# ScalarE instead of VectorE writes the one-hot operand of each expert's bias product

## What is computed

```python
u = xb @ w1[e] + b1[e]
glu = jnp.minimum(u[:, ::2], SWIGLU_LIMIT)
lin = jnp.clip(u[:, 1::2], -SWIGLU_LIMIT, SWIGLU_LIMIT)
a = glu * jax.nn.sigmoid(SWIGLU_ALPHA * glu) * (lin + 1.0)
return a @ w2[e] + b2[e]
```

## Time and profile before

| | before |
|---|---|
| median of 3 runs (lowest to highest) | 3779.34 us (3778.82 to 3779.49) |
| the profiled execution's own time | 3781.95 us |
| its span | 3780.1 us |
| TensorE, VectorE, ScalarE busy over the span | 91%, 55%, 46% |
| one unit of the mixture | some 36.5 us, 34 of them |

### The profile page before, as it was taken

One profiled execution on the slowest core, in us unless ns is written; L12 is line 12 of the kernel. 1 busy time (PEld: TensorE's weight loads), 2 busy tenths in 40 slices (PEclk: granted clock), 3 DMA queues, 4 the chain that ended last, 5 costly groups with the idle time before them and its releaser, 6 DMA issues. The chain is left out here.

```text
span 3780.1 us, 55651 instructions
## 1 busy us (share of the span) xinstructions
PE 3444.3 (91%) x20889; PEld 2782.7 (74%) x20889; DVE 2088.5 (55%) x2469; ACT 1755.3 (46%) x2286; POOL 1040.9 (28%) x435
## 2 busy tenths in 40 slices
PE   7989999969999999999999687899998886779997
PEld 4877777648888888888887574688877765668876
DVE  2320111259999999999999236411240263246665
ACT  3222333137787777777777325222242342033333
POOL 2334233202322223232231220244432300024443
PEclk9999999969999999999999798799998966789999
DMA  8223433249999999999999327123231200013221
GB/s 270 80 67 95 138 114 123 78 152 366 366 381 370 370 380 365 383 366 375 376 365 374 116 82 267 45 78 100 95 95 56 96 1 5 7 46 101 100 86 43
DMA packets 245432, 696.84 MB, mean 184 GB/s; under 512 B 17846, under 2 KB 149802, under 8 KB 186652
## 3 DMA queue, kind: packets, MB, share of 16 engines
q1 hardware_dynamic: 234956, 657.73, 46.7%
q0 software_dynamic: 9936, 36.18, 3.6%
q10 hardware_dynamic: 384, 0.65, 0.0%
HBM read 668.73 MB, written 30.23 MB: 185 GB/s over the span
## 5 line engine op out<-in xcount | busy, mean ns | idle before, releaser
L311 POOL TENSOR_TENSOR split_w<-ring,split_w 128x1024 fp32r<-128x1024 f32 (+1 forms) x294 | 698.2, 2375 | 1736.7 <-ACT split_w L306 1589.5
L1811 DVE TENSOR_TENSOR moe_low<-ring,moe_high 128x2048 fp32r<-128x2048 f32 x408 | 929.1, 2284 | 23.6 <-ACT moe_high L1802 23.4
L1802 ACT ACTIVATE moe_high<-ring 128x1024 fp32r<-128x1024 f32 x810 | 827.7, 1058 | 103.7 <-PE psum L2054 101.8
L306 ACT ACTIVATE split_w<-ring 128x1024 fp32r<-128x1024 f32 (+1 forms) x294 | 304.7, 1036 | 1034.6 <-PE psum L376 649.2
L2050 PE MATMUL psum<-moe_high,moe_xe 128*128 128x512 f32 x2176 | 586.9, 391 | 0.0
L2050 PEld LDWEIGHTS psum<-moe_high,moe_xe 128*128 128x128 f32 x2176 | 410.4, 189 | 85.2
L1962 POOL DMA_INDIRECT moe_y_rows<-moe_ye,moe_target x34 | 197.4, 5806 | 696.2 <-DVE moe_ye L1866 696.2
L376 PE MATMUL psum<-pair,split_w 128*128 128x512 f32 x1584 | 364.7, 393 | 13.0 <-PEq L128 6.2
L376 PEld LDWEIGHTS psum<-pair,split_w 128*128 128x128 f32 x1584 | 300.5, 190 | 76.5 <-issue 9.1
L376 PE MATMUL psum<-b_pair,split_w 128*128 128x512 f32 x1440 | 334.7, 394 | 12.9 <-PEq L840 7.1
L2054 PE MATMUL psum<-moe_low,moe_xe 128*128 128x512 f32 x1088 | 337.3, 391 | 0.0
(11 more groups left out here) (589 smaller groups left out, 4336.9 us busy)
## 6 DMA issues: line engine op xcount, KB each, us to landing
ring<-in_w_experts SPq DMA_DIRECT2D x408, 1024.0 KB, 7.5
ring<-in_w_mod SPq DMA_DIRECT2D x48, 1024.0 KB, 7.2
ring<-in_w_in SPq DMA_DIRECT2D x39, 1024.0 KB, 5.3
ring<-in_w_up SPq DMA_DIRECT2D x33, 1024.0 KB, 5.1
ring<-in_w_in SPq DMA_DIRECT2D x44, 512.0 KB, 5.1
ring<-in_w_down SPq DMA_DIRECT2D x20, 1024.0 KB, 5.0
ring<-in_w_gate SPq DMA_DIRECT2D x11, 1024.0 KB, 5.2
ring<-in_w_out SPq DMA_DIRECT2D x8, 1024.0 KB, 6.0
```

The lines of the kernel that those rows point to most:

```text
L306: self.nc.scalar.activation(high, raw, ACT.Copy).then_inc(self.K.rounded, 1)
L311: self.nc.gpsimd.tensor_tensor(low, raw, high.bitcast(F32), ALU.subtract).then_inc(self.K.split, 1)
L1802: self.nc.scalar.activation(self.B["high"][:, j % HALVES, :], self.raw(j), ACT.Copy).then_inc(self.high, 1)
L1811: self.nc.vector.tensor_tensor(flat("low"), self.K.ring[:, self.ring_slot(j // 2), :], flat("high").bitcast(F32), ALU.subtract).then_inc(s ...
```

## The change

A table `owns`, 128 x 48, is made once, ahead of the loop: column v has a one in the partitions whose bias row belongs to the expert of unit v, and zero elsewhere. ScalarE then writes `esel` of a unit as a 128x128 tile of ones scaled by column v of `owns`, right after `act_xe` and ahead of high(25). VectorE's comparison and the PSUM column are gone. `owns` is allocated first among the tiles of the mixture, so the others move by 192 bytes in each partition. Before the loop, ScalarE waits for `made` (VectorE's set-up) and writes `esel` of unit 0 after its first `act_xe`; nothing waits on the new semaphore `esel_due`.

```diff
-    def dve_esel(self, ve, v):
-        B = self.B
-        self.nc.vector.tensor_scalar(B["esel"][:, :], B["ps_row"].to_broadcast([P, CAP]),
-                                     B["unit_f"][:, bass.ds(v, 1)], None, ALU.is_equal).then_inc(self.esel, 1)
...
         low(22)
-        if ahead:
-            self.dve_esel(ve, u + 1)
         low_of_turned(3)
...
+    def act_esel(self, sc, v):
+        B = self.B
+        self.nc.scalar.activation(B["esel"][:, :], self.K.ones[:, 0:CAP], ACT.Copy, scale=B["owns"][:, bass.ds(v, 1)])\
+            .then_inc(self.esel, 1)
...
         if ahead:
             self.act_xe(sc, u + 1)
+            self.act_esel(sc, u + 1)
         high(25, 26, 27, 28, 29)
...
+        owns = sb("owns", [P, EXPERTS + SPILLS + 1])
...
-                nc.vector.tensor_copy(B["ps_row"], slots[:, 5:6])
+                nc.vector.tensor_scalar(B["owns"], unit_f[:, :], slots[:, 5:6], None, ALU.is_equal)
...
-                X.dve_esel(ve, 0)
                 X.dve_pick(ve, 0, True)
...
                 X.act_xe(sc, 0)
+                sc.wait_ge(made, 1)
+                sc.sem_inc(X.esel_due, 1)
+                X.act_esel(sc, 0)
                 with sc.Fori(0, n1) as u:
```

More of the change, by code:

```diff
@@ L1779, in __init__ @@
         self.picked, self.placed, self.read, self.staged = n_("picked"), n_("placed"), n_("read"), n_("staged")
-        self.esel = n_("esel")
+        self.esel, self.esel_due = n_("esel"), n_("esel_due")
         self.gathered, self.scattered = K.moe_gathered, K.moe_scattered
@@ L2102, in mixture @@
              "ps_gate": table[:, 128:384].rearrange("p (t s e) -> p t s e", s=2, e=EXPERTS),
-             "ps_row": table[:, 384:385], "ps_place": table[:, 388:392], "from_end": from_end[:, :],
+             "owns": owns[:, :], "ps_place": table[:, 388:392], "from_end": from_end[:, :],
              "unit_e": unit_e, "unit_f": unit_f, "unit_at": unit_at, "gates_f": gates_f,
```

## The result

The changed kernel is slower by 0.18%: ratio 1.0018, 95% interval 1.0010 to 1.0025, medians of 15 runs 3786.29 and 3779.49 us, so 6.8 us where 4.7 were forecast. That lies within the forecast range and on the forecast side, and under the 0.2% that counted as a difference.

The account below looks back on a forecast made before the run. A ring through TensorE, ScalarE and VectorE, closing in two units, was taken to set the pace: 17 x 0.29 = 4.9 us, less 0.26, gives +4.7 us, 3784.0 us for the median; range 3777 to 3790.

Parts of the forecast that it names:

- VectorE's gain is 0: Removing the comparison (0.26 us of VectorE) ahead of low(24) only lengthens the wait for high(25); gain 0 in the loop.
- rival B: Faster: VectorE's load sets the pace, 0.26 us less shortens each of 34 units: -8.8 us, 3770.5 us; chance 0.08.
- ScalarE's copy takes 0.29 us: Scaled copy between token matrix and high(25), where ScalarE has no idle time: 0.29 us, range 0.22 to 0.5.
- It costs half of that in each unit: The copy's 0.29 us enters a ring spanning two units, so each unit costs 0.145 us more, 4.9 us in all.
- the ring through two units: turn(3), high(24), low(24), turned group 2's low part, back to turn(3): 73.03 us for two units, 36.52 for one.
- the one-unit ring through turn(1): high(24), high(25), low(24), group 0's low part, turn(1), half 18: 36.34 us, 0.18 slack, becoming 36.63 against 36.66.
- The ring's sum as evidence: Four parts, 36.32 + 3.30 + 33.26 + 0.15, sum to 73.03 us; 36.52 a unit equals the measured pace.
- rival A: Slower: the one-unit ring through turn(1) sets the pace, every unit pays in full; 3789.3 us at a = 0.5; chance 0.17.
- a: Time the added copy takes of ScalarE between token matrix and high(25): taken as 0.29 us, range 0.22 to 0.5.
- The next unit's first matmul is far off: Token matrix is ready 0.52 us ahead of the next unit's first matmul; with 0.145 more, VectorE keeps ahead.
- Set-up, moved tiles, table loads: Set-up saves 0.26 us, its other changes 0; 192-byte tile move 0, some 3 us either way; extra table loads unlikely, 0.03.

Follow-up runs that it names:

- e4_no_dve: Kernel before with VectorE's comparison left out of the loop, all units adding the first unit's bias: 36.53 us a unit, ratio 1.0001.
- e1_hidden: Changed kernel with ScalarE's copy moved into ScalarE's idle time, between high(21) and the unit's last sigmoid: 36.54 us a unit, ratio 1.0006.
- e13_xe_both_before: Kernel before, comparison kept, token matrix written earlier on both ScalarE and VectorE: 36.18 us a unit, ratio 0.9964.
- e12_xe_both_after: Changed kernel with the token matrix written earlier on both ScalarE and VectorE: 36.17 us a unit, ratio 0.9964.
- e5_both: Kernel before, comparison kept, with ScalarE's copy added in the change's place into an unread spare tile: 36.76 us a unit, ratio 1.0020.
- e10_after_pick: Changed kernel with VectorE's pick for the unit after next moved ahead of low(24): 36.53 us a unit, ratio 0.9994.
- after: The changed kernel itself, against the kernel before: 36.77 us a unit, ratio 1.0018.
- e3_twice: Changed kernel with ScalarE's copy made twice in the same place, the first into a spare tile: 37.06 us a unit, ratio 1.0049.

## Why the prediction was right, and where not

- *VectorE's gain is 0.* Right, shown by `e4_no_dve` and `e1_hidden`: the row that decided it was the wait directly behind the comparison, against a busy share of 98%. The rule of the Trainium skill that spoke for rival B (Perfetto Trace Analysis, Identifying the Most-Contended Engine), to optimize the engine with the highest occupancy first, would have led one to take the comparison off a nearly full engine. Here the gain of that is nil, and stays nil in `e13_xe_both_before` against `e12_xe_both_after`, where VectorE is busy 397.7 of 400 us.
- *ScalarE's copy takes 0.29 us, with nothing around it to hide it.* Right to the hundredth, register address included; `e5_both` has the cost without the rest of the change.
- *It costs half of that in each unit*, the ring through two units. **This is the term that was mis-sized**: 0.145 us forecast, 0.23 measured. The two-unit ring was there, as the alternating distances show, but in the changed kernel the one-unit ring through turn(1) came first. The prediction gave it 0.18 us of slack, the distance from VectorE's release to the matmul's start, 0.33, less a floor of 0.15. But the turn starts with a weight load. In that same unit of the kernel before it is here:

```profile
1510.57 0.34 PEld L2041 LDWEIGHTS psum<-identity,hT 128*128 128x128 f32 x2
```

  1510.57 is 0.12 us after the release at 1510.45. The floor is to be had at turn(3) of the next unit, where the load does wait; the release there ended at 1558.73, 0.11 us ahead of it:

```profile
1558.84 0.20 PEld L2041 LDWEIGHTS psum<-identity,hT 128*128 128x128 f32 x2 [0.66 <-DVE hT L1894]
```

  So the load had almost no slack where its matmul still had 0.18. In the changed kernel that load waits openly, and the matmul is now at its floor, 0.16 us after the release at 1518.53:

```profile
1518.12 0.41 DVE L1874 TENSOR_TENSOR moe_aT<-psum,moe_aT 128x256 fp32r<-128x256 f32 x1
...
1518.65 0.20 PEld L2040 LDWEIGHTS psum<-identity,hT 128*128 128x128 f32 x2 [0.33 <-issue]
1518.69 0.41 PE L2040 MATMUL psum<-identity,hT 128*128 128x128 f32 x2
```

  Late loads also lengthen TensorE's stretch from turn(1)'s matmul to the start of high(24), which the prediction took as fixed: 1522.17 - 1510.78 = 11.39 us before, 1530.17 - 1518.69 = 11.48 after, and 11.37 and 11.49 on average over the units. Most of it stands behind turn(2), in the kernel before and the changed one:

```profile
1516.49 0.37 PEld L2041 LDWEIGHTS psum<-identity,hT 128*128 128x128 f32 x2
1516.72 0.38 PE L2041 MATMUL psum<-identity,hT 128*128 128x128 f32 x2
1516.86 1.18 PE L2050 MATMUL psum<-moe_high,moe_aT 128*128 128x512 f32 x4
```

```profile
1524.51 0.26 PEld L2040 LDWEIGHTS psum<-identity,hT 128*128 128x128 f32 x2
1524.63 0.38 PE L2040 MATMUL psum<-identity,hT 128*128 128x128 f32 x2
1524.85 1.19 PE L2049 MATMUL psum<-moe_high,moe_aT 128*128 128x512 f32 x4
```

  The load comes 0.12 us ahead of its transpose instead of 0.23, and the product starts 0.22 us after the transpose instead of 0.14. The ring in the changed kernel is then, on average over the units, 3.59 (ScalarE) + 21.54 (VectorE, low(24) to the release at turn(1)) + 0.15 + 11.49 (TensorE) = 36.77 us, all of the measured distance. Less the copy's 0.29 it stood at 36.48: its slack was in effect 0.06 us, and not 0.18.

- *The ring's sum as evidence.* "The ring accounts for the whole of it" says less than it seems to. The four parts add up to the distance from one turn(3) to the next (36.56) plus that from one high(24) to the next (36.47), whatever waited in between, so their sum had to match the pace. What showed a ring was the waits, and then the experiments.
- *The number.* That the forecast time stood is no evidence for the halving: the interval of the measured time takes in both sizes. The sign named for rival A, a distance of 36.8 with waits at turn(1), is nearly what the trace shows.
- *Rival A* was this mechanism, with the wrong threshold: it was to set in at a = 0.36; from 36.48 + a = 36.54 + a/2 it sets in at about 0.12, an estimate that no run tested.
- *The next unit's first matmul is far off*, 0.52 us: right for the change itself, where no row has a wait there. But this slack, too, was measured from the matmul's start. Its load comes 0.28 us after the token matrix was ready at 1528.90:

```profile
1529.18 0.19 PEld L2061 LDWEIGHTS psum<-moe_b,moe_esel 128*128 128x128 f32 x1
```

  The expectation of `e10_after_pick` took this ring to be out of the way, and it was the one that bound.
- *Set-up, moved tiles, table loads*: no cost seen, as taken. The set-up's 0.26 us is far below what the run-in varies, and nothing shows it.

## What to carry to other kernels

On a nearly full engine, work that stands directly ahead of that engine's own wait was free here, and moving it onto the engine whose chain ends the wait made it cost; so look at what ends the next wait, not at busy shares. Where several engines hand a unit of work round, write each ring with its length and the number of units through which it closes; the cost of an added step is its time divided by that number, and the shortest slack decides which ring counts. Measure slack to the first instruction that waits, which at these turns is the weight load and not the matmul, and do not take the stretch behind it as fixed once that instruction is late.

## What the runs showed of the hardware

A weight load that comes late cost TensorE time even where its own matmul was on time: at turn(2) the load came 0.12 us ahead of the transpose instead of 0.23, the transpose followed the matmul ahead of it after 0.23 us as before, and the product behind started 0.08 us later. TensorE's stretch from turn(1)'s matmul to the start of high(24) was 11.48 to 11.50 us on average in the three kernels in which that load was late (`after`, `e5_both`, `e3_twice`) and 11.37 to 11.38 in the others with the turns in the same place. The three pairs of transposes of turns 0 to 2, each moved one product later, cost some 0.07 us more in each unit (36.32 against 36.25); two of them then stand between two products of one group. A column operand at an address from a register made ScalarE's copy no longer to speak of: 0.398 us here, 0.39 in the nearest row with a fixed address, of another function.
